# All six pieces of an expert's matrices in rounded halves, and its first matrices loaded as 2 x 1 MB

## The reference, cut to what matters

```
scores = sigmoid(h @ router_w); idx = the 8 best experts of the 4 best groups
wts    = scores[idx] / sum * 2.5
expert(e, rows) = (silu(rows @ w1[e]) * (rows @ w3[e])) @ w2[e]      # 1024 -> 256 -> 1024
out[token] = sum over its 8 experts of wts * expert(e, token)  + shared expert
```

## Time and profile before

| | |
|---|---|
| median of 3 runs | 2858.55 us |
| profiled execution, its own time | 2863.36 us |
| its span (first to last instruction) | 2861.1 us |
| TensorE, VectorE, ScalarE, GpSimd busy | 95%, 62%, 44%, 8% of the span |
| mean granted clock of TensorE | 0.975 |
| the expert loop, 61 of its steps | 804.62 to 1418.81 us |
| moved by DMA | 442 MB, mean 155 GB/s |

### The profile page before, as it was taken

How to read it: one execution, slowest core, us unless ns; L and a number is a source line. 1 busy time by engine, 2 the same in 40 slices (tenths; PEclk the granted TensorE clock), 3 DMA queues, 4 the chain that set the end, 5 groups by cost and what they waited for, 6 DMA issues and landing times.

```text
span 2861.1 us, 42808 instructions
## 1 busy us (share of the span) xinstructions
PE 2706.0 (95%) x17240; PEld 2121.7 (74%) x17240; DVE 1779.2 (62%) x3174; ACT 1261.9 (44%) x2232; POOL 227.5 (8%) x212
## 2 busy tenths in 40 slices
PE   6998998889999999999978989999999998999998
PEld 6887777774777777777736766888888775888887
DVE  5257876676688888888745896432334688433333
ACT  3332554221277777777713337322223328422222
POOL 0000000000022222222200120000000030000000
PEclk9999997999999999999989999999999999999999
DMA  6210002424489999999874331314224340323321
GB/s 238 89 59 23 1 3 77 124 62 163 160 309 359 360 361 359 362 372 355 339 299 159 108 77 32 119 51 139 74 81 133 96 107 12 100 77 96 118 69 63
DMA packets 186546, 442.44 MB, mean 155 GB/s; under 512 B 21283, under 2 KB 110694, under 8 KB 167014
## 3 DMA queue, kind: packets, MB, share of 16 engines
q1 hardware_dynamic: 161862, 396.59, 38.6%
q0 software_dynamic: 24480, 43.04, 5.1%
HBM read 426.43 MB, written 38.29 MB: 162 GB/s over the span
## 4 chain that ended last, share of the span: by engine, by line
PE 78%; DVE 9%; DMA 6%; ACT 4%; issue 2%; SPq 0%; ACTq 0%; DVEq 0%; POOLq 0%
PE ps L296 19%; PE ps L298 19%; PE ps L297 19%; DMA ring<-in_ew 5%; PE ps L2534 3%; PE ps L2036 2%; PE ps L1519 2%; PE ps L2563 1%; PE ps L2781 1%; PE ps L2241 1%; DVE Pb L3530 1%; DMA yr<-y_rows 1%; DVE spA L2467 1%; DVE spB L2467 1%; PE ps L3419 1%
## 5 line engine op out<-in xcount | busy, mean ns | idle before, releaser
L2993 DVE TENSOR_TENSOR wf<-ring,wf 128x1024 fp32r<-128x1024 f32 (+1 forms) x152 | 181.7, 1196 | 312.3 <-ACT wf L2989 312.0
L2989 ACT ACTIVATE wf<-ring 128x1024 fp32r<-128x1024 f32 (+1 forms) x152 | 156.8, 1033 | 347.9 <-PE ps L298 347.9
L296 PE MATMUL ps<-hxh,wf 128*128 128x512 f32 (+1 forms) x736 | 279.9, 380 | 2.3 <-DVE hxl L3156 2.3
L297 PE MATMUL ps<-hxl,wf 128*128 128x512 f32 (+1 forms) x736 | 279.5, 380 | 0.0
L298 PE MATMUL ps<-hxh,wf 128*128 128x512 f32 (+1 forms) x736 | 279.5, 380 | 0.0
L2467 DVE TENSOR_TENSOR spA<-ring,spA 128x1024 fp32r<-128x1024 f32 x196 | 234.0, 1222 | 57.1 <-ACT spA L2462 56.3
L2462 ACT ACTIVATE spA<-ring 128x1024 fp32r<-128x1024 f32 x196 | 202.8, 1072 | 47.1 <-DMA ring<-in_ew 44.7
L296 PEld LDWEIGHTS ps<-hxh,wf 128*128 128x128 f32 x736 | 138.4, 188 | 28.9 <-DVE hxl L3156 2.7
L297 PEld LDWEIGHTS ps<-hxl,wf 128*128 128x128 f32 x736 | 138.4, 188 | 26.3
L298 PEld LDWEIGHTS ps<-hxh,wf 128*128 128x128 f32 x736 | 138.4, 188 | 25.9
L2467 DVE TENSOR_TENSOR spB<-ring,spB 128x1024 fp32r<-128x1024 f32 x129 | 157.2, 1219 | 0.4 <-ACT spB L2462 0.4
(11 more groups left out here) (630 smaller groups left out, 6555.0 us busy)
## 6 DMA issues: line engine op xcount, KB each, us to landing
ring<-in_ew SPq DMA_DIRECT2D x65, 2048.0 KB, 13.1
ring<-in_ew SPq DMA_DIRECT2D x65, 1024.0 KB, 7.7
ring<-in_w_in SPq DMA_DIRECT2D x17, 2048.0 KB, 8.7
ring<-in_w_gate SPq DMA_DIRECT2D x20, 1024.0 KB, 5.5
ring<-in_w_up SPq DMA_DIRECT2D x20, 1024.0 KB, 8.0
ring<-in_w_down SPq DMA_DIRECT2D x16, 1024.0 KB, 5.1
adaw<-in_ada_w SPq DMA_DIRECT2D x24, 512.0 KB, 6.3
ring<-in_w_out SPq DMA_DIRECT2D x6, 2048.0 KB, 8.5
```

What stands on the lines that cost most here:

```text
L296: pe.matmul(o, lhs[0], rhs[0], start=start, stop=False)
L297: pe.matmul(o, lhs[0], rhs[1], start=False, stop=False)
L2989: act.activation(item_part(n)[0], item_raw(n), ACT.Copy).then_inc(*w_hi.inc(n))
L2993: v.tensor_tensor(item_part(n)[1], item_raw(n), f(item_part(n)[0]), ALU.subtract).then_inc(*w_lo.inc(n))
```

## The change

The second half of `w2` becomes piece 5. ScalarE makes its high half into `w5h` in stage 3, right after piece 4, and GpSimd its low half into `w5l`, in a new stage 3 of its own list, which stands between the scatter and the gather. Stage 4 on TensorE is then twelve split matmuls in place of six and two float32 ones; the second six wait for GpSimd's half. The copy to `hdT` goes. `yb` has two buffers and not three, and so ScalarE waits for the scatter of two experts ago. The 2 MB of first matrices are loaded as two transfers of 1 MB: the first waits only for the low half of piece 1 of the expert that had the slot, and the second for that of piece 3, as the whole did; ScalarE waits for the second before piece 2.

```diff
--- before.py
+++ after.py
...
-    sb("gap", [128, D], c=b1)
+    w5h = sb("w5h", [128, D], R32, c=b1)
...
-    yb = sb("yb", [128, 3, D], c=m4)
+    yb = sb("yb", [128, 2, D], c=m4)
+    w5l = sb("w5l", [128, D], R32, c=m4)
...
+    wk13b = Loads([sem(f"d_ring{k}") for k in range(2)], [1] * 64)
...
-    k_act = Signal(sem("expert_scalar"), split_keys((1, 2, 3, 4), {1: "t0 t1", 2: "silu", 3: "hd hf", 4: "y"}))
+    k_act = Signal(sem("expert_scalar"), split_keys((1, 2, 3, 4), {1: "t0 t1", 2: "silu", 3: "hd", 4: "y"}))
...
+    p_lo5 = Signal(sem("gather_zero"), range(NX))
...
     def piece(e, j):
+        if j == 5:
+            return [w[:, :].rearrange("p (k n) -> p k n", k=2) for w in (w5h, w5l)]
         m = 2 if j == 4 else 4 if j == 2 and e else j
...
     def piece_raw(e, j):
-        if j == 4:
-            return wv2[(e + 1) % 2].rearrange("p (k n) -> p k n", k=2)[:, :, 0:512]
+        if j >= 4:
+            return wv2[(e + 1) % 2].rearrange("p (k n) -> p k n", k=2)[:, :, 512 * (j - 4):512 * (j - 4) + 512]
...
         for j in js:
+            if e and j == 2:
+                act.wait_ge(*wk13b.val(e - 1))
             if (e, j) == (0, 4):
                 act.wait_ge(*p_use.val((0, 2)))
+            elif j == 5:
+                if e:
+                    act.wait_ge(*k_pe.val(("y1", e - 1)))
...
             elif e < NX:
-                sp.wait_ge(*p_lo.val((e - 2, 3)))
+                sp.wait_ge(*p_lo.val((e - 2, 1)))
...
             if e < NX:
-                sp.dma_start(wv13[(e + 1) % 2], weights(e, 0, 4096)).then_inc(*wk13.inc(e + 1))
+                sp.dma_start(wv13[(e + 1) % 2][:, 0:2048], weights(e, 0, 2048)).then_inc(*wk13.inc(e + 1))
+                if e > 1:
+                    sp.wait_ge(*p_lo.val((e - 2, 3)))
+                sp.dma_start(wv13[(e + 1) % 2][:, 2048:4096], weights(e, 2048, 4096)).then_inc(*wk13b.inc(e - 1))
...
-        for k, n in [(0, 0)] + [(k, n + (k == 0)) for k, n in steps((0, 4))]:
-            if k == 0:
+        for k, n in [(0, 0)] + [(k, n + (k == 0)) for k, n in steps((0, 3, 4))]:
+            if k == 3:
+                g.wait_ge(*p_hi.val((n, 5)))
+                g.tensor_tensor(piece(n, 5)[1], piece_raw(n, 5), f(piece(n, 5)[0]), ALU.subtract).then_inc(*p_lo5.inc(n))
+            elif k == 0:
...
-                scatter(g, n, n % 3).then_inc(*d_sca.inc(n))
+                scatter(g, n, n % 2).then_inc(*d_sca.inc(n))
...
             if k == 4:
-                w2 = wv2[(n + 1) % 2].rearrange("p (k n) -> p k n", k=2)
-                pe.wait_ge(*wk2.val(n + 1))
                 if n:
                     pe.wait_ge(*k_act.val(("y", n - 1)))
                 pe.wait_ge(*k_dve.val(("hl", n)))
-                pe.wait_ge(*p_lo.val((n, 4)))
-                for j in range(2):
-                    m = mm3(pe, ps[5][:, :], [hdp[:, q, j, :] for q in range(2)], [w[:, j, :] for w in piece(n, 4)], start=(j == 0), stop=(j == 1))
-                m.then_inc(*p_use.inc((n, 4)))
-                pe.wait_ge(*k_act.val(("hf", n)))
-                for j in range(2):
-                    m = pe.matmul(ps[6][:, :], hdT[:, j, :], w2[:, j, 512:1024], start=(j == 0), stop=(j == 1))
+                for q in range(2):
+                    pe.wait_ge(*(p_lo5.val(n) if q else p_lo.val((n, 4))))
+                    for j in range(2):
+                        m = mm3(pe, ps[5 + q][:, :], [hdp[:, x, j, :] for x in range(2)], [w[:, j, :] for w in piece(n, 4 + q)],
+                                start=(j == 0), stop=(j == 1))
+                    if q == 0:
+                        m.then_inc(*p_use.inc((n, 4)))
                 m.then_inc(*k_pe.inc(("y1", n)))
...
-                if n >= 3:
-                    act.wait_ge(*d_sca.val(n - 3))
-                act.activation(yb[:, n % 3, :].rearrange("p (q n) -> p q n", q=2), psa[:, 5:7, :], ACT.Copy).then_inc(*k_act.inc(("y", n)))
+                if n >= 2:
+                    act.wait_ge(*d_sca.val(n - 2))
+                act.activation(yb[:, n % 2, :].rearrange("p (q n) -> p q n", q=2), psa[:, 5:7, :], ACT.Copy).then_inc(*k_act.inc(("y", n)))
...
                 act.activation(hdp[:, 0, :, :], hT_, ACT.Copy).then_inc(*k_act.inc(("hd", n)))
-                act.activation(hdT[:, :, :], hT_, ACT.Copy).then_inc(*k_act.inc(("hf", n)))
-                pieces_act(act, n, (4,))
+                pieces_act(act, n, (4, 5))
```

More of the change, by code:

```diff
@@ L2434, in _program @@
     g_hg = Signal(sem("gather_zero"), ["set"])
+    p_lo5 = Signal(sem("gather_zero"), range(NX))
     MADE = [(0, j) for j in range(4)] + [x for k, n in steps((2, 3)) for x in
-                                         ([(n, 4)] if k == 3 else [(n + 1, j) for j in range(4) if n + 1 < NX])]
+                                         ([(n, 4), (n, 5)] if k == 3 else [(n + 1, j) for j in range(4) if n + 1 < NX])]
     USED = [x for k, n in steps((2, 4)) for x in ([(n, 4)] if k == 4 else [(n, j) for j in range(4)])]
     p_hi = Signal(sem("piece_hi"), MADE)
-    p_lo = Signal(sem("piece_lo"), MADE)
+    p_lo = Signal(sem("piece_lo"), [x for x in MADE if x[1] < 5])
     p_use = Signal(sem("piece_mm"), USED)
     def piece(e, j):
+        if j == 5:
+            return [w[:, :].rearrange("p (k n) -> p k n", k=2) for w in (w5h, w5l)]
         m = 2 if j == 4 else 4 if j == 2 and e else j
@@ L2538, in expert_pe @@
                 if n:
-                    pe.wait_ge(*k_act.val(("hf", n - 1)))
+                    pe.wait_ge(*k_act.val(("hd", n - 1)))
                     pe.wait_ge(*k_dve.val(("hl", n - 1)))
@@ L2599, in expert_dve @@
             if k == 3:
-                v.wait_ge(*k_act.val(("hf", n)))
+                v.wait_ge(*k_act.val(("hd", n)))
                 v.tensor_tensor(hdp[:, 1, :, :], ps[4][:, 0:256].rearrange("p (q s) -> p q s", q=2), f(hdp[:, 0, :, :]),
@@ L2664, in over_pe @@
         pe.wait_ge(*k_dve.val(("hd2", NX - 1)))
-        pe.wait_ge(*k_act.val(("hf", NX - 1)))
+        pe.wait_ge(*k_act.val(("hd", NX - 1)))
         pe.wait_ge(*k_dve.val(("hl", NX - 1)))
```

## The result

The changed kernel takes 2869.9 us (median of 20 runs, 2862.2 to 2873.7) against 2861.9 for the kernel before (median of 20, 2855.2 to 2866.1, on the same chip). The ratio is 1.0028, 95% interval 1.002 to 1.0035: 8 us slower, where 2.4 us less and a median of 2856 had been forecast (from three runs with a median of 2858.6). The time is inside the forecast range of 2836 to 2876, the direction is not.

A forecast was written before the change was run, and what follows sets the result against it. The prediction took the fullest DMA engines' load queue, 10.14 us a step, as the bound, with TensorE within 2%. Terms 0 - 2.3 - 0.6 + 0.5 = -2.4 us gave a median of about 2856, range 2836 to 2876.

The forecast's parts named there:

- What bounds the kernel: Expert loop: fullest DMA engines need 10.14 us a step, TensorE 9.98; the two within 2%.
- the queue: Weight loads in the expert loop wait behind the fullest DMA engines, 10.14 us a step by landings.
- the estimate of 10.1 us a step: Half of the DMA engines: 1/16 of the weights plus 16 rows, 262 KB at 25.9 KB/us.
- TensorE, 0.32 us a step, hidden: Four fp32 passes (1.72 us) become six split matmuls (1.40); the gain goes into a wait for transposed hidden rows: 0.
- Two transfers, -2.3 us by a shorter chain and no cost of their own: First-matrix loads: landing to `hd` falls from 4.9 to 2.6 us, counted once; the extra transfer costs 0.
- its bounds of 0 to 2.2: First-matrix loads: excess of two halves over one whole, us a step, from queued to each waited for.
- GpSimd's subtraction, 2.7 us, hidden: Sixth low half on GpSimd ends at 1112.6, TensorE needs it after 1114.3: hidden by 1.7 us, 0.
- the rival's first mechanism, the gather: GpSimd gather issued after the subtraction, landing late; TensorE waits 0.3 to 0.5 us a step: 2880, chance 0.16.
- its idle time at a landing: VectorE: this and transposed-row work fall beside GpSimd's subtraction, so little lockout is expected.
- L2467 over 1.22 us: VectorE's low-half subtraction running longer, a sign that GpSimd gets in the way; that case's chance 0.16.
- The last two experts, -0.6 and +0.5: Loop end: shorter TensorE steps after the last landing, -0.6 us; sixth low half on the last step's path, +0.5.

The follow-up runs named there:

- without the lock: Changed kernel with the sixth low half left out (zeros) and the first matrices loaded in one 2 MB transfer: 2857.5 us, ratio 0.9997 to the kernel before.
- freeing the queue: Kernel before with an expert's tokens placed in turn at slots 0, 64, 1, 65, over both partition halves: 2854.7 us, ratio 0.9972.
- both together: Changed kernel with the sixth low half left out and tokens placed in turn at slots 0, 64, 1, 65: 2833.0 us, ratio 0.9895.
- dealt rows: An expert's tokens placed in turn at slots 0, 64, 1, 65: 0.9972 on the kernel before, 0.9895 without the sixth low half, 1.0020 on the changed kernel.
- beneath the halves: Changed kernel without the sixth low half, first matrices in two 1 MB transfers against one of 2 MB: 2863.9 us (1.0014) against 2857.5 (0.9997).
- beside memsets: Changed kernel with GpSimd's subtraction replaced by three memsets in a row, the sixth low half zero: 2866.6 us, ratio 1.0023.

## Why the prediction was wrong

*What bounds the kernel.* Right. The kernel before has two limits within 2% of one another, and the queue is the later one: taking 0.34 us a step off TensorE without the lock gives little (0.9997, at most 4 us), freeing the queue gives 8 us on the kernel before, and both together give 30 (0.9895, without the sixth low half). By the Trainium skill ("DMA: Bandwidth & Descriptors", The descriptor swizzle) partitions 0 to 63 of a 128-partition transfer belong to engines 0 to 7; the estimate of 10.1 us a step that went with it would make dealt rows the cure, and the runs agree: dealt steps of 9.83 and 9.49 us. Which engine a packet is on no row here shows. The six undealt steps of 60.3 to 60.4 us put the queue's need at 10.06 us a step, where the prediction had 10.14.

*TensorE, 0.32 us a step, hidden.* Right in size (0.34) and, without the lock, right in being hidden.

*Two transfers, -2.3 us by a shorter chain and no cost of their own.* Wrong in sign by the medians: +3.7 us alone (1.0000 to 1.0025), and +4.9 beneath the halves, each hardly clear of noise; in the profiled loops it is +3.6 and +1.3. The rows said that 2 MB land in 7.6 us at best and 1 MB in 4.9, and the prediction took the excess as 0 since transfers in a queue overlap. A cost of 0.02 to 0.08 us a step is within its bounds of 0 to 2.2. By the Trainium skill ("SBUF — State Buffer", Summary: rules for kernel authors) one DMA is to be preferred to several; these runs agree in sign, by no more than that. Whether it sits in the packets (twice as many, of 8 KB) or in the order and time of the issues, which changed with them, is open; no run separates these. The shorter chain brought nothing that could be seen.

*GpSimd's subtraction, 2.7 us, hidden.* This is the step that failed. The duration was right (2.62), and so was its start behind the scatter; the gather behind it was not late for anyone, so the rival's first mechanism, the gather, did not happen: GpSimd issued it late at 1110.14 and 1122.17 us, and it landed in 5.0 to 10.4. What failed is the sentence that VectorE's transposed-row work and its idle time at a landing would fall beside the subtraction, "so I expect little of it". The first half of it came true: of GpSimd's 152 us in 815 to 1400 us, 61 have L2630 beside them, which keeps its time. But L2630 is 1.27 us of a subtraction of 2.5, and of the rest 75 us have L2477 beside them and only some 13 have VectorE idle. GpSimd's trigger is the sixth high half on ScalarE. VectorE then has the fifth low half before L2630 and the next expert's first one behind it, and one of these two is caught in nearly every step: 62 pieces, 55 us more in all than at 1.22 each. L2467 over 1.22 us is the sign that the prediction had named for this case, but it had priced the case by a late gather.

The trace before had the means for a price: VectorE busy 8.7 us of 10.07, so 1.4 us of room on the mean, against an exclusion of up to 2 us. In four steps of six the lengthening is about 0.5 us, and the room takes it. In the two where it is 1.0 and 2.0 VectorE has list work too, which the mean of 8.7 hides, and these are the two steps that grew: from 9.94 to 10.04 us and from 9.88 to 11.46.

*The last two experts, -0.6 and +0.5.* The last two spacings of the evictions are 9.36 and 8.99 us before and 8.67 and 8.09 after, 1.6 us less in the two profiled executions, where 0.1 less had been forecast.

*The size of the loss.* It is the difference of two limits and not the sum of costs. VectorE under the lock needs 61.0 us for six steps, the queue 60.3 to 60.4. The loop from the first to the last eviction of `yb` (64 steps) goes from 643.4 us to 648.3 in the two profiled executions, +4.9, of the 8 that the runs show; without the subtraction it is 641.5. The rest, some 3 us, lies outside the loop: the first eviction comes 5.0 us later (809.66 and 804.63), and what follows the last is 1.4 us shorter. Before the loop the code does the same work, and its first eviction comes between 802.7 and 809.7 in the profiled executions of all the kernels here, so this part can't be assigned.

By the Trainium skill ("SBUF — State Buffer", Who interferes with whom) two-input VectorE instructions and GpSimd instructions that read SBUF lock one another out. The runs agree: 1.22 us becomes 1.7 to 3.4 beside a subtraction (2.6 us), and stays 1.22 beside memsets, which read nothing. The prediction named the rule and then discounted it by an overlap that it had not laid out in time: it covers half of the subtraction.

## What to carry to other kernels

Before work is moved to GpSimd, lay its start beside VectorE's timeline of that step: if two-input work in SBUF stands there, count GpSimd's time as VectorE's, and judge by the fullest step of a period and not by the mean. Where two limits are within a few per cent, lowering one is worth little until the other falls (at most 4 us for TensorE alone, 8 for the queue alone, 30 for both, though in a kernel that leaves the sixth low half out), so look for the pair. Where rows fill a tile only from its first partitions, try dealing them over both halves; here it was one constant and 8 us. That some DMA engines are full while others have room is what it was meant to cure; no row shows it by engine.

## What the runs showed of the hardware

- A VectorE subtraction of two SBUF inputs of 1024 fp32 columns (1.22 us) that begins while GpSimd subtracts two SBUF inputs (2.59 to 2.63 us) ends one piece after GpSimd does: 3.10 and 3.11 us. GpSimd's takes 3.12 when VectorE is first. These ends fit a turn for whole instructions and not a shared rate. VectorE's subtractions with an input in PSUM took their usual time beside it (L2630 1.27 us for two), and memsets on GpSimd left the piece at 1.22.
- The mean DMA share does not tell the limit. Without the sixth low half the queue was the limit at 0.94 and 363 GB/s, and with rows dealt the same kernel ran at 0.98 and 378 GB/s, with TensorE never waiting. The dealt kernel before ran at 0.95 with TensorE as its limit.
- Two transfers of 1 MB in place of one of 2 MB in a full queue cost 0.02 to 0.08 us a step of 3 MB (3.7 and 4.9 us by the medians and ratios, 3.6 and 1.3 in the profiled loops; each near the noise), and nothing to be seen in one with room (0.0003).
